# A fused attention and expert-layer kernel: the compressed branch's first product as rows of blocks, and the first loads in another order

## The chip, the cores and the metric

The kernel is one program on one NeuronCore of a Trainium2 chip. The core has five engines with their own instruction streams: TensorE (PE; its weight loads are shown as PEld), VectorE (DVE), ScalarE (ACT), GpSimdE (POOL) and SyncE (SP). They wait for each other by semaphores. DMAs are issued from the queues of SP, ACT and POOL. The metric is the time of one execution on the device, in microseconds (us). Three runs of the kernel before took 2562.18 to 2570.23, with a median of 2567.21.

## The reference, cut to what matters

Two blocks run one after the other on X of 512 tokens x 1024 features, all in float32. The first is attention with three branches and a gated MLP. The second is a short convolution beside a gated recurrence, and then an expert layer: each token picks 128 experts of 16384 and reads their rows of two tables. The change touches the compressed part of the third attention branch. There each of two key/value groups is cut in blocks of 32 tokens with stride 16, and each block goes through a two-layer MLP:

```
def compress_blocks(kv, pe, w1, w2):        # kv: (1, 512, 2, 64)
    n_cmp = (S - 32) // 16 + 1              # 31 blocks
    blocks = kv[:, idx] + pe
    flat = blocks.transpose(0, 1, 3, 2, 4).reshape(1, n_cmp, 2, 32 * 64)
    return jax.nn.gelu(flat @ w1) @ w2      # w1: 2048 x 256, w2: 256 x 64
kc = compress_blocks(k_cmp, cmp_pe, k_w1, k_w2)
vc = compress_blocks(v_cmp, cmp_pe, v_w1, v_w2)
...
merged = g[:, :, 0] * (y_a @ w_pa) + g[:, :, 1] * (y_b @ w_pb) + g[:, :, 2] * (y_c @ w_pc)
```

`kc` and `vc` are then the keys and values of one more attention, and `g` is a sigmoid of a product with 3072 columns of `w_in` (the gates).

## The kernel before, in words

The 512 tokens are worked in two groups, g = 0 and 1, of 256 (two tiles of 128). For each group the program runs `project`, `attend`, `merge`, `mlp`, `mixer` and `queries`. During group 1 the engines also work off the expert steps of group 0: a "job" is one gather of 128 rows of 4 KB by POOL's queue and one pass of DVE over them. The experts of group 1 make up the rest of the program, from about 1780 us on.

Weights stream from memory through a ring of four buffers of 1 MB, W0 to W3, in the order of `weight_tiles`, all from SP's queue. Tile i is asked for when the last use of tile i - 4 is done. X's two tiles for group 0 are loaded by `load_x(0)` as the first DMAs of ACT's queue, then come COLS (biases and gains) and FIX (identity, a row of numbers, two constants). SP issues the first weight tile at once and the others after X is there.

`norm` squares X on ACT (two halves for each tile), takes the root, and PE turns X while it scales it (L660). ACT needs a table of functions for Square and another for Sqrt. The projections follow: a "feature" is eight products of a 128x128 weight with 256 tokens.

`compressed(g)` makes the first product of the MLP. FB holds the blocks in turned form: 128 partitions x 30 columns for each of 16 parts of the 2048 rows (in group 1, 32 columns, and the buffer is XS0). For each of keys and values (kv) and each half m of the 256 hidden columns, 16 products are summed with a 128x128 piece of the weights as the part that stands in the array and FB's 30 columns moving past it; ACT applies the gelu straight into HID, where the hidden index lies on the partitions, as the second product (KCT, VCB) needs it. These 64 products a group all run before (g = 1) or around (g = 0) the first attention unit.

`attend(g)` then goes through 44 units (22 heads x 2 tiles, u = 0 to 43). PE's order at unit u is: scores of u, turning of the probabilities of u - 2, values of u - 3, and then the pieces that the table `BESIDE` puts beside u: a "gate" piece is one feature and a tanh on ACT. The coroutine `compressed` advances one `yield` a unit. In group 1 the expert steps are spread over this by `state["spent"]`: each product adds what it is reckoned to take, and as much expert work is taken off; 5.0 is added for each of the four sums of the compressed product. KEPT = 16 jobs are held back for the end. Each engine works off the same list up to the point that PE's order sets (`catch_up`).

## Time and profile before

| | |
|---|---|
| three runs, median (range) | 2567.21 (2562.18 to 2570.23) us |
| profiled execution, its own time | 2564.7 us |
| its span | 2562.9 us |
| busy: PE, PEld, DVE | 2218.9, 1560.6, 1564.3 us |
| busy: ACT, POOL | 617.7, 943.8 us |
| instructions | 24943 |
| moved by DMA | 683.55 MB, 267 GB/s |

A busy PE is not a PE at its peak: a matmul's end is modelled, and the granted clock (PEclk) says at how much of its full rate the array ran. A float32 product stands in the trace as two records, so "x16" is eight products. PEclk is 1.0 at 2.4 GHz and 0.5 at 1.2 GHz; numbers between are stretches that hold both. The trace shows the instruction's line; L633 is the helper `mm` of all products, so the names of the operands tell them apart.

### The profile page before, as it was taken

To read this page: it belongs to the slowest core of one execution; us is meant where nothing else is said; L and a number is where in the kernel's file an instruction comes from. 1 tells how busy PE (TensorE), PEld (TensorE's weight loads), DVE (VectorE), ACT (ScalarE), POOL (GpSimd) and SP (SyncE) were. 2 spreads that over 40 slices of the span, in tenths; PEclk is the share of its full clock that TensorE was granted. 3 is DMA by queue.
4 is the path that set the end of the run, shared out by engine and by line. 5 is a ranking of instruction groups with operands and counts; after the bars stand their busy time and mean duration, and the time that the engine had idled before them with its cause. 6 is when DMAs were issued, how large, how long until landed. Compare 5 with 4: busy or idle time off the path is not lost.

```text
span 2562.9 us, 24943 instructions
## 1 busy us (share of the span) xinstructions
PE 2218.9 (87%) x8844; PEld 1560.6 (61%) x8844; DVE 1564.3 (61%) x3488; ACT 617.7 (24%) x1763; POOL 943.8 (37%) x772
## 2 busy tenths in 40 slices
PE   7999999999989899998999989778433599999992
PEld 6877768856858777676688637647333544444441
DVE  0122321202436957899777766857989988666667
ACT  1223211202211121432111213111799600000000
POOL 0000000000002534555456564624677246555554
PEclk9979999999989986998999999889655899999996
DMA  5432344444436987898899998957789489999997
GB/s 166 141 99 75 107 140 156 156 148 137 132 98 239 330 283 255 291 323 295 324 337 401 387 399 303 355 198 269 264 305 357 134 325 407 407 409 409 409 409 288
DMA packets 296689, 683.55 MB, mean 267 GB/s; under 512 B 21234, under 2 KB 134130, under 8 KB 296308
## 3 DMA queue, kind: packets, MB, share of 16 engines
q0 software_dynamic: 110592, 402.70, 42.3%
q1 hardware_dynamic: 179904, 266.54, 30.3%
q10 hardware_dynamic: 6068, 12.71, 1.5%
q8 instruction: 70, 1.15, 0.2%
q14 instruction: 55, 0.45, 0.1%
HBM read 679.78 MB, written 2.10 MB: 266 GB/s over the span
## 4 chain that ended last, share of the span: by engine, by line
PE 43%; DVE 25%; DMA 17%; POOL 8%; issue 4%; ACT 2%; ACTq 0%; DVEq 0%; POOLq 0%
PE bank L633 41%; DMA SLOT<-in_peer_v,EI 8%; DVE SLOT L1753 8%; POOL SLOT L2298 8%; DMA SLOT<-in_peer_u,EI 8%; DVE ACC L1767 3%; PE bank L660 2%; DVE X L1767 1%; DVE H L1685 1%; DVE PB L1306 1%; DVE OH L1652 1%; DVE OH L1657 1%; DVE EX L1660 1%; DMA W<-in_cmp_k_w 1%; PE bank L785 1%
## 5 line engine op out<-in xcount | busy, mean ns | idle before, releaser
L2298 POOL DMA_INDIRECT SLOT<-in_peer_u,EI x512 | 640.7, 1251 | 1364.8 <-DVE EI L1669 828.4
L633 PE MATMUL bank<-HT,W 128*128 128x256 f32 x4032 | 917.9, 388 | 16.5 <-issue 6.6
L633 PEld LDWEIGHTS bank<-HT,W 128*128 128x128 f32 x4032 | 776.6, 194 | 136.2 <-issue 17.2
L1753 DVE CUSTOM_DVE_ANT_0 SLOT<-SLOT,H 128x1024 f32<-128x1024 f32 x384 | 454.8, 1221 | 50.7 <-DMA SLOT<-in_peer_u,EI 49.3
L2298 POOL DMA_INDIRECT SLOT<-in_peer_v,EI x256 | 302.9, 1183 | 231.8 <-DVE ACC L1767 96.0
L633 PE MATMUL bank<-H,SPREAD 128*128 128x512 f32 x680 | 302.7, 596 | 7.1 <-DMA H<-in_peer_v 7.0
L633 PEld LDWEIGHTS bank<-H,SPREAD 128*128 128x128 f32 x680 | 125.9, 190 | 178.2 <-issue 133.0
L1767 DVE SCALAR_TENSOR_TENSOR X<-SLOT,AA,X 128x1024 f32<-128x1024 f32 x128 | 164.4, 1284 | 76.9 <-DMA SLOT<-in_peer_v,EI 74.1
L1753 DVE CUSTOM_DVE_ANT_0 SLOT<-SLOT,ACC 128x1024 f32<-128x1024 f32 x128 | 154.5, 1223 | 64.4 <-DMA SLOT<-in_peer_u,EI 64.1
L1767 DVE SCALAR_TENSOR_TENSOR ACC<-SLOT,AA,ACC 128x1024 f32<-128x1024 f32 x128 | 164.1, 1282 | 19.8 <-DMA SLOT<-in_peer_v,EI 13.7
L633 PE MATMUL bank<-JK,SPREAD 128*128 128x512 f32 x344 | 157.1, 599 | 3.6 <-DMA JK<-in_peer_v 3.6
L633 PE MATMUL bank<-W,UT 128*128 128x512 f32 x352 | 151.4, 592 | 0.0
L633 PEld LDWEIGHTS bank<-JK,SPREAD 128*128 128x128 f32 x344 | 63.2, 190 | 93.2 <-issue 65.8
L633 PEld LDWEIGHTS bank<-W,UT 128*128 128x128 f32 x352 | 66.9, 190 | 83.3 <-issue 83.2
L633 PE MATMUL bank<-H 128*128 128x128 f32 x296 | 58.4, 362 | 60.3 <-ACT H L2210 52.2
L633 PE MATMUL bank<-JK 128*128 128x128 f32 x216 | 47.4, 388 | 63.9 <-ACT JK L2210 56.6
L1827 ACT ACTIVATE HT<-X 128x512 f32<-128x512 f32 x40 | 24.9, 624 | 294.0 <-DVE X L1430 150.6
L633 PEld LDWEIGHTS bank<-H 128*128 128x128 f32 x296 | 50.8, 260 | 67.6 <-ACT H L2210 53.2
L1961 ACT ACTIVATE PB<-PB,NM 128x128 f32<-128x128 f32 (+2 forms) x88 | 48.7, 554 | 155.8 <-DVE NM L1306 155.1
L1306 DVE CUSTOM_DVE_ANT_0 PB<-bank,BIAS 128x128 f32<-128x128 f32 (+2 forms) x72 | 34.2, 476 | 84.3 <-PE bank L633 82.3
L633 PEld LDWEIGHTS bank<-JK 128*128 128x128 f32 x216 | 40.8, 282 | 70.3 <-ACT JK L2210 57.8
L660 PE MATMUL bank<-XS,X 128*128 128x128 f32 x256 | 40.7, 334 | 49.2 <-DVE SS L1152 31.8
(304 smaller groups left out, 2389.4 us busy)
## 6 DMA issues: line engine op xcount, KB each, us to landing
W<-in_w_in SPq DMA_DIRECT2D x68, 1024.0 KB, 5.7
W<-in_w_up SPq DMA_DIRECT2D x44, 1024.0 KB, 6.0
H<-in_peer_v SPq DMA_DIRECT2D x85, 512.0 KB, 6.8
JK<-in_peer_v SPq DMA_DIRECT2D x43, 512.0 KB, 6.8
W<-in_w_down SPq DMA_DIRECT2D x20, 1024.0 KB, 6.3
W<-in_peer_wq SPq DMA_DIRECT2D x16, 1024.0 KB, 5.8
W<-in_w_o SPq DMA_DIRECT2D x8, 1024.0 KB, 6.1
W<-in_w_out SPq DMA_DIRECT2D x8, 1024.0 KB, 6.2
```

Source lines behind the costliest of these rows:

```text
L633: return e.matmul(out, lhsT, rhs, start=start, stop=stop)
L660: k = e.matmul(pb[:, c * P:(c + 1) * P], lhsT=X[:, t, at:at + P], rhs=DIAG[t], start=True, stop=True)
L785: k = e.transpose(pb[:, j * P:(j + 1) * P], PB[u % 3][:, j * P:(j + 1) * P], IDENT)
L1306: e.tensor_tensor_reduce(out=PB[u % 3][:, 0:wd], in0=ps("score", g, u)[:, 0:wd], in1=t, scale=-1.0, scalar=3.0e38, op0=ALU.add, op1=ALU.mi ...
L1652: e.tensor_tensor(OH, HL.unsqueeze(2).to_broadcast([P, 64, 16]), IOTA[:, 0:16].unsqueeze(1).to_broadcast([P, 64, 16]), ALU.is_equal).then_inc(
L1657: e.tensor_tensor(one_hot, one_hot, IF.unsqueeze(2).to_broadcast([P, 4, 16, 16]), ALU.mult).then_inc(*d_exp.mark("pick", t, h))
L1660: e.tensor_reduce(EX.rearrange("p l s j -> p (l s j)"), OH, AX, ALU.add).then_inc(*d_exp.mark("add", t, h))
L1685: k = e.tensor_scalar(left[:, i, :], IOTA, TURNED[t][:, 1, n:n + 1], TURNED[t][:, 0, n:n + 1], ALU.is_equal, ALU.mult)
L1753: e.tensor_tensor_reduce(out=x, in0=x, in1=NORMED[t], scale=1.0, scalar=0.0, op0=ALU.mult, op1=ALU.add, accum_out=AA[t % 2][:, k:k + 1]).t ...
L1767: e.scalar_tensor_tensor(SUM[t], x, AA[t % 2][:, k:k + 1], SUM[t], ALU.mult, ALU.add).then_inc(*d_exp.mark("job", t, i))
L1961: e.activation(s, s, ACT.Exp, bias=NM[:, n, il:il + 1], scale=-1.0, accum_out=LS[:, n, il:il + 1]).then_inc(*a_att.mark("exp", g, u))
L2298: e.indirect_dma_start(out=SLOT_OF[s], out_offset=None, in_=a["peer_v_2"] if i >= P else a["peer_u_2"], in_offset=bass.IndirectOffsetOnAxi ...
```

## The change

The first product of the compressed branch is turned round: FB's 30 (32) columns are now what stands in the array, and 256 columns of the weights move past, so one sum of 16 products gives a 30 x 256 result for each kv. ACT's gelu writes it to a new buffer HB, rows of blocks. PE turns it in two pieces of 128 (function `turned`), and ACT copies them into HID. The turning for kv = 0 comes behind the products of kv = 1, the one for kv = 1 a `yield` later, before the second product. The four additions of 5.0 to `spent` are gone.

The eight gates of the first branch stand beside units 0, 1, 2, 4, 6, 8, 11, 15 in place of 1, 4, 6, 8, 10, 13, 16, 19, in both groups.

X's first tiles are issued from SP's queue ahead of the first weight tile. ACT's queue issues FIX and then COLS. ACT takes a root of a 1.0 that DVE writes at its start, before it waits for anything that was loaded.

```diff
@@ -174,7 +174,7 @@
 
 ALPHA = 24
 BESIDE = {}
-for _u, _p in ([(u, ("gate", 0, m)) for m, u in enumerate((1, 4, 6, 8, 10, 13, 16, 19))]
+for _u, _p in ([(u, ("gate", 0, m)) for m, u in enumerate((0, 1, 2, 4, 6, 8, 11, 15))]
                + [(13, ("turned", 0, 0))] + [(21 + m // 2, ("part", 0, m)) for m in range(8)]
                + [(23 + m, ("gate", 1, m)) for m in range(8)] + [(27, ("turned", 1, 0))]
                + [(31 + m // 3, ("part", 1, m)) for m in range(8)]
@@ -398,6 +398,7 @@
         PCT.append(buf("PCT", 2, GB, P, at=at + 384))
         CT.append(buf("CT", 2, GB * 96, at=at + 896))
         CM.append(buf("CM", 2, GB * 96, at=at + 1280))
+        HB = [[buf(f"HB{j}", 256, at=at + 1664 + 256 * j) for j in range(2)]]
         FBF.append(XS[0])
         FW.append(XS[1][:, 0:2 * T].rearrange("p (a b) -> p a b", a=2))
         W2.append([XS[1][:, 512 + 128 * j:640 + 128 * j].rearrange("p (a b) -> p a b", a=2) for j in range(2)])
@@ -405,6 +406,7 @@
         PCT.append(buf("PCT_1", 2, GB, P, at=jk_at + 384))
         CT.append(buf("CT_1", 2, GB * 96, at=nf_at))
         CM.append(buf("CM_1", 2, GB * 96, at=nf_at + 384))
+        HB.append([buf("HB_1", 256, at=nf_at + 768), XS[1][:, 768:1024]])
         BV = XS[0][0:1, 0:914]
 
 
@@ -695,23 +697,33 @@
                 c0, nb = (0, 15) if g == 0 else (15 + 16 * (g - 1), 16)
                 ntot = c0 + nb
                 FB = FBF[g].rearrange("p (a b c) -> p a b c", a=2, b=16)[:, :, :, 0:2 * nb]
+
+                def turned(kv):
+
+                    pb, _ = take(("hidt", g, kv), (a_cmp, ("hidt", g, kv)))
+                    w.wait_ge(*a_cmp["hid", g, kv])
+                    for m in range(2):
+                        k = e.transpose(pb[:, m * 32:m * 32 + 2 * nb], HB[g][kv][0:2 * nb, m * P:(m + 1) * P],
+                                        IDENT[0:2 * nb, 0:2 * nb])
+                    k.then_inc(*p_cmp.mark("hidt", g, kv))
+
                 for kv in range(2):
-                    (i0, w0), (i1, w1) = tile(), tile()
-                    for m in range(2):
-                        pb, _ = take(("hid", g, kv, m), (a_cmp, ("hid", g, kv, m)))
-                        w.wait_ge(*d_cmp["fb", g, 1])
-                        for c in range(16):
-                            k = mm(pb[:, 0:2 * nb], (w0, w1)[c // 8][:, c % 8, m * P:m * P + P], FB[:, kv, c, :],
-                                   c == 0, c == 15)
-                        state["spent"] += 5.0
-                        k.then_inc(*p_cmp.mark("hid", g, kv, m))
-                    last_use(i0, p_cmp, "hid", g, kv, 1)
-                    last_use(i1, p_cmp, "hid", g, kv, 1)
+                    halves = (tile(), tile())
+                    pb, _ = take(("hid", g, kv), (a_cmp, ("hid", g, kv)))
+                    w.wait_ge(*d_cmp["fb", g, 1])
+                    for c in range(16):
+                        k = mm(pb[0:2 * nb, 0:256], FB[:, kv, c, :], halves[c // 8][1][:, c % 8, :], c == 0, c == 15)
+                    k.then_inc(*p_cmp.mark("hid", g, kv))
+                    for i, _ in halves:
+                        last_use(i, p_cmp, "hid", g, kv)
+                    if kv:
+                        turned(0)
                     yield
+                turned(1)
                 w.wait_ge(*cw_in["cw", g, 1])
                 for q in range(2):
                     pb, _ = take(("kct", g, q), (d_cmp, ("kct", g, q)))
-                    w.wait_ge(*a_cmp["hid", g, 1, 1])
+                    w.wait_ge(*a_cmp["hidt", g, 1])
                     lo, hi = q * 31 + c0, q * 31 + ntot
                     mm(pb[0:64, 0:nb], W2[g][0][:, 0, :], HID[:, 0, 0, lo:hi], True, False)
                     mm(pb[0:64, 0:nb], W2[g][0][:, 1, :], HID[:, 0, 1, lo:hi], False, True).then_inc(
@@ -1769,6 +1781,7 @@
                 if k == P - 1:
                     out(t)
 
+            e.memset(SS[:, 31:32], 1.0).then_inc(*d_set.mark("one"))
             for v in (AH, UH, STP, VCB):
                 e.memset(v, 0.0)
             e.memset(ONER[0:1, :], 1.0)
@@ -1911,14 +1924,24 @@
             def compressed(g):
                 c0, nb = (0, 15) if g == 0 else (15 + 16 * (g - 1), 16)
                 ntot = c0 + nb
+
+                def turned(kv):
+                    catch_up("hidt", g, kv)
+                    w.wait_ge(*p_cmp["hidt", g, kv])
+                    for m in range(2):
+                        k = e.copy(HID[:, kv, m, :].rearrange("p (q c) -> p q c", q=2)[:, :, c0:ntot],
+                                   ps("hidt", g, kv)[:, m * 32:m * 32 + 2 * nb].rearrange("p (q c) -> p q c", q=2))
+                    k.then_inc(*a_cmp.mark("hidt", g, kv))
+
                 for kv in range(2):
-                    for m in range(2):
-                        catch_up("hid", g, kv, m)
-                        w.wait_ge(*p_cmp["hid", g, kv, m])
-                        e.activation(HID[:, kv, m, :].rearrange("p (q c) -> p q c", q=2)[:, :, c0:ntot],
-                                     ps("hid", g, kv, m)[:, 0:2 * nb].rearrange("p (q c) -> p q c", q=2),
-                                     ACT.Gelu_apprx_tanh).then_inc(*a_cmp.mark("hid", g, kv, m))
+                    catch_up("hid", g, kv)
+                    w.wait_ge(*p_cmp["hid", g, kv])
+                    e.activation(HB[g][kv][0:2 * nb, :], ps("hid", g, kv)[0:2 * nb, 0:256],
+                                 ACT.Gelu_apprx_tanh).then_inc(*a_cmp.mark("hid", g, kv))
+                    if kv:
+                        turned(0)
                     yield
+                turned(1)
                 yield
                 yield
                 for par in range(2):
@@ -2250,9 +2273,10 @@
                     w.wait_ge(*d_exp["sum", t, 1])
                     out(t)
 
-            load_x(0)
+            e.dma_start(FIX, con("ident", 258)).then_inc(*small_in.mark("fix"))
             e.dma_start(COLS, a["cols"]).then_inc(*small_in.mark("cols"))
-            e.dma_start(FIX, con("ident", 258)).then_inc(*small_in.mark("fix"))
+            w.wait_ge(*d_set["one"])
+            e.activation(SS[:, 30:31], SS[:, 31:32], ACT.Sqrt)
             for t_small in ("cols", "fix"):
                 w.wait_ge(*small_in[t_small])
             for g in range(NG):
@@ -2303,6 +2327,9 @@
 
         def sync(e, real):
             w = Waits(e, real)
+            xv = a["x"].rearrange("(t p) d -> t p d", p=P)
+            for t in range(GB):
+                e.dma_start(X[:, t, :], xv[t]).then_inc(*x_in[t].mark("x", 0, t))
             for i, (parts, width) in enumerate(tiles):
                 if 1 <= i < RING:
                     for t in range(GB):
```

What follows shows how the instructions of the engines moved. First PE at the compressed product of group 0, before (FB is the block buffer, W1 to W3 and W0 are the ring's buffers; the operand that moves stands first, so `FB,W` has the weights in the array):

```order
L633 MATMUL bank0<-FB_109,W1_55 128x30 x8
L633 MATMUL bank0<-FB_109,W2_56 128x30 x8
L633 MATMUL bank1<-FB_109,W1_55 128x30 x8
L633 MATMUL bank1<-FB_109,W2_56 128x30 x8
L810 MATMUL bank2<-FIX_52,FC_63 128x4 x2
L633 MATMUL bank3<-FB_109,W3_57 128x30 x8
L633 MATMUL bank3<-FB_109,W0_54 128x30 x8
L633 MATMUL bank4<-FB_109,W3_57 128x30 x8
L633 MATMUL bank4<-FB_109,W0_54 128x30 x8
L633 MATMUL bank5<-KF_60,QF_97 128x128
L633 MATMUL bank6<-FC_63,SEL_62 128x256
L633 MATMUL bank7<-HID_64,CW0_111 64x15 x2
```

After, the same place up to the second attention unit (HB is the new buffer, FIX holds the identity, CW the second weights, HT,W a gate's feature):

```order
L635 MATMUL bank0<-W1_55,FB_109 30x256 x8
L635 MATMUL bank0<-W2_56,FB_109 30x256 x8
L822 MATMUL bank1<-FIX_52,FC_63 128x4 x2
L635 MATMUL bank2<-W3_57,FB_109 30x256 x8
L635 MATMUL bank2<-W0_54,FB_109 30x256 x8
L706 MATMUL bank3<-FIX_52,HB0_117 128x30 x2
L635 MATMUL bank4<-KF_60,QF_97 128x128
L635 MATMUL bank5<-FC_63,SEL_62 128x256
L635 MATMUL bank6<-HT_50,W1_55 128x256 x8
L706 MATMUL bank7<-FIX_52,HB1_118 128x30 x2
L635 MATMUL bank0<-HID_64,CW0_111 64x15 x2
L635 MATMUL bank1<-HID_64,CW0_111 64x15 x2
```

64 products of 30 moving columns became 32 of 256, two pairs of turnings were added, and a gate's feature stands between the first unit's scores and the second turning.

ACT at the start of the program, before:

```order
L2179 DMA X_49<-in_x 128x1024 x2
L2254 DMA COLS_51<-in_cols 128x219
L2255 DMA FIX_52<-in_con 128x258
L1827 ACT_TABLE_LOAD
L1827 ACTIVATE HT_50,SS_53<-X_49 128x512 x2
L1835 ACTIVATE SS_53<-SS_53,FIX_52 128x1 x2
L1837 ACT_TABLE_LOAD
L1837 ACTIVATE SS_53<-FIX_52 128x1
```

ACT at the start, after:

```order
L2276 DMA FIX_52<-in_con 128x258
L2277 DMA COLS_51<-in_cols 128x219
L2279 ACT_TABLE_LOAD
L2279 ACTIVATE SS_53<-SS_53 128x1
L1840 ACTIVATE HT_50,SS_53<-X_49 128x512 x2
L1848 ACTIVATE SS_53<-SS_53,FIX_52 128x1 x2
L1850 ACTIVATE SS_53<-FIX_52 128x1
```

One of the two table loads is gone, and the other stands ahead of the squares of X; X's own DMA is no longer ACT's.

ACT around the same place of group 0, after (in the order before, four ACTIVATE HID<-bank rows of 128x2x15 stood there, and the first gate behind the second unit's exponential):

```order
L1939 ACT_TABLE_LOAD
L1939 ACTIVATE HB0_117<-bank0 30x256
L1972 ACTIVATE BIAS0_99<-DIST_98,FIX_52 128x256
L1939 ACTIVATE HB1_118<-bank2 30x256
L1932 COPY HID_64<-bank3 128x2x15 x2
L1984 ACT_TABLE_LOAD
L1984 ACTIVATE PB0_101,LS_91<-PB0_101,NM_90 128x128
L2062 ACTIVATE GATE_107<-bank6,COLS_51 128x256
L1932 COPY HID_64<-bank7 128x2x15 x2
L1984 ACTIVATE PB1_102,LS_91<-PB1_102,NM_90 128x256
```

Two gelus on 30 x 256 and four copies take the place of four gelus on 128 x 30, and the second pair of copies stands behind the first gate.

## Rows read from the trace of the kernel before

**Rows 1.** Timeline, the first 16 us: start us, us, engine line op [idle before]

```profile
9.56 1.28 ACT L1827 ACT_TABLE_LOAD   x1 [9.56 <-DMA FIX<-in_con]
...
12.57 1.28 ACT L1837 ACT_TABLE_LOAD   x1
13.87 0.20 ACT L1837 ACTIVATE SS<-FIX 128x1 f32<-128x1 f32 x1
...
15.58 0.16 DVE L1152 RECIPROCAL SS<-SS 128x1 f32<-128x1 f32 x1 [5.41 <-ACT SS L1842]
```

**Rows 2.** DMA issues from 0 to 20 us: KB each, median us to landing

```profile
X<-in_x ACTq DMA_DIRECT2D x2, 512.0 KB, 5.9
...
FIX<-in_con ACTq DMA_DIRECT2D x1, 129.0 KB, 7.2
```

**Rows 3.** Timeline, PE, 117 to 153 us

```profile
117.71 11.01 PE L633 MATMUL bank<-FB,W 128*128 128x30 f32 x64
...
128.96 13.86 PE L633 MATMUL bank<-FB,W 128*128 128x30 f32 x64
...
146.73 6.00 PE L633 MATMUL bank<-HT,W 128*128 128x256 f32 x16
```

**Rows 4.** Stretches: busy us (x) of PE, PEld, DVE, ACT, POOL, granted clock, DMA share, GB/s

```profile
117.00:143.00 26.00, 26.00 (x139) 25.86 (x138) 0.17 (x1) 4.21 (x9) 0.00 (x0) 0.57 0.47 145
143.00:165.00 22.00, 21.57 (x84) 15.98 (x85) 7.58 (x35) 5.63 (x19) 0.00 (x0) 0.66 0.30 96
165.00:200.00 35.00, 32.18 (x142) 24.47 (x141) 8.90 (x46) 12.48 (x47) 0.00 (x0) 0.84 0.19 61
200.00:250.00 50.00, 49.50 (x241) 39.09 (x240) 13.54 (x68) 18.38 (x68) 0.00 (x0) 0.97 0.28 83
...
980.00:1010.00 30.00, 26.91 (x83) 16.93 (x84) 25.42 (x72) 5.87 (x16) 10.04 (x9) 0.61 0.66 221
1010.00:1200.00 190.00, 175.59 (x791) 129.59 (x789) 180.30 (x496) 63.72 (x163) 100.92 (x84) 0.91 0.86 296
```

**Rows 5.** Timeline, ACT taking a feature off PE

```profile
34.09 0.47 ACT L1894 ACTIVATE KF<-bank,COLS 128x256 f32<-128x256 f32 x1 [2.98 <-PE bank L633]
```

**Rows 6.** Timeline, PE with 4 columns of the array in use

```profile
83.62 2.32 PE L633 MATMUL bank<-HT,W 128*4 128x256 f32 x10
```

**Rows 7.** Timeline, group 1: SP's issue, PE's products, DVE's wait

```profile
939.30 7.01 SPq L2314 DMA_DIRECT2D W<-in_cmp_v_w  x2
...
950.03 27.49 PE L633 MATMUL bank<-XS,W 128*128 128x32 f32 x128 [5.51 <-DMA W<-in_cmp_k_w]
977.90 1.01 PE L633 MATMUL bank<-HID,XS 128*64 128x16 f32 x8 [0.38 <-ACT HID L1918]
978.52 0.78 DVE L1225 COPY KCT<-bank 64x16 f32<-64x16 f32 x4 [10.60 <-PE bank L633]
```

**Rows 8.** DMA issues from 938 to 948 us: KB each, median us to landing

```profile
W<-in_cmp_v_w SPq DMA_DIRECT2D x2, 1024.0 KB, 18.7
```

**Rows 9.** Timeline at the end of the mixer of group 1

```profile
1696.70 29.86 PE L633 MATMUL bank<-W,MIX 128*128 128x512 f32 x64 [9.32 <-DVE O L1567]
...
1716.29 0.69 DVE L1407 TENSOR_TENSOR X<-X,bank 128x512 f32<-128x512 f32 x1 [18.03 <-PE bank L633]
```

**Rows 10.** The stretch behind that idle time, in the columns of rows 4

```profile
1696.00:1701.00 5.00, 4.30 (x5) 1.85 (x6) 2.19 (x5) 0.00 (x0) 0.94 (x1) 0.50 0.15 30
```

**Rows 11.** The page, part 5, a job on DVE: busy, mean ns, idle before

```profile
L1753 DVE CUSTOM_DVE_ANT_0 SLOT<-SLOT,H 128x1024 f32<-128x1024 f32 x384 | 454.8, 1221 | 50.7 <-DMA SLOT<-in_peer_u,EI 49.3
```

**Rows 12.** Timeline, PE, group 0: the gates at units 13 and 19

```profile
197.59 6.14 PE L633 MATMUL bank<-HT,W 128*128 128x256 f32 x16
...
215.21 3.67 PE L633 MATMUL bank<-HT,W 128*128 128x256 f32 x16
```

**Rows 13.** Timeline, ACT, group 1: the gates at units 13 and 19

```profile
1061.67 0.47 ACT L2039 ACTIVATE KF<-bank,COLS 128x256 f32<-128x256 f32 x1 [2.72 <-PE bank L633]
...
1085.19 0.47 ACT L2039 ACTIVATE KF<-bank,COLS 128x256 f32<-128x256 f32 x1
```

## The prediction

> **What bounds the kernel now.** I read the stretches of the timeline first, then the chain of waits, then the timeline of single places. The reader should see that the change touches three places and that another thing sets the pace in each.
>
> At the start PE has nothing to do until ACT has squared X. ACT is idle until FIX has landed, loads a table at 9.56, a second one at 12.57, and DVE gets the roots at 15.58 [rows 1]. In group 0 PE is busy all the time from 117 to 143, but at a granted clock of 0.57, and until 200 the clock is 0.66 and 0.84 [rows 4]. Here PE alone sets the end: DVE and ACT are busy for less than 8 of 22 us from 143 to 165. In group 1 the same products stand behind a wait for their weights, and DVE, which has the expert jobs to do, has run out of them and waits 10.60 us for the second product [rows 7]. From 1010 to 1200 DVE is busy for 180.30 of 190 us [rows 4]: there DVE is the bound, and PE's gains count only if DVE starts sooner.
>
> **The start.** X and FIX are what ACT waits for. X took 5.9 us to land (the mean of two), FIX 7.2 us though it has a quarter of the bytes, since it was issued behind X and beside the first weight tile [rows 2]. Afterwards FIX goes first on ACT's queue and X first on SP's, ahead of the weight tile. The rows bound when both are there: not before X's 5.9 us (I take 6.6 us on the clock, since the second half of X is issued half a us later), and not after 9.56. The squares then start at about 6.6 in place of 10.85 (9.56 and 1.28 and their overlap), and the table load at 12.57, which holds the row behind it to 13.87, goes: 4.25 + 1.3 = 5.5 us. The new load waits for nothing but DVE's first write and lies beside the DMAs. The least is that FIX comes no sooner and only both loads go from the path, 2.6 us; the most is 7. SP's tiles 1 to 3 still wait for X, which is sooner there, and PE needs tile 0 at about 18, so no weights are late.
>
> The Trainium skill (ScalarE: Activation LUTs, What ACT_TABLE_LOAD costs) gives about 2.66 us for a switch of tables, half of it a drain. By that the two loads would be worth 5.3 us. Here the ACTIVATE behind the load at 12.57 starts 1.30 us later [rows 1], so the trace does not bear the drain out, and the sum goes by 1.3. The skill (Trainium Kernel Development and Optimization, Key Constraints) also says that DMAs from SP's and ACT's queues share the same 16 engines and interleave, so that another queue by itself brings X no sooner. By that alone the squares would start where FIX lands, and only the order of issue would help; the trace has no row that parts the two.
>
> **The product, group 0.** 64 products go, which ran from 117.71 to 142.8: 25.05 us, 0.39 us each, with the products for CQ between them [rows 3]. 32 with 256 moving columns come. The price of one at full clock is a feature's: ACT waits 2.98 us for one and works on it for 0.47, so one comes off every 3.45 us, eight products, 0.431 us each [rows 5]. That is 13.8 us; the columns standing in the array are 30 and not 128, and a feature with only 4 of them takes no less or more (ten records in 2.32 us, two a product, make 0.46) [rows 6]. Added are four turnings of 30 rows (0.25 us, bounded by the 0.39 us of an old product each, and nothing), CQ (0.2), and a wait of about 0.6 us at the second product, since the turning of kv = 1 needs a copy on ACT that stands behind a gate. 25.05 - 13.8 - 0.25 - 0.2 - 0.6 = 10.2 us. The weights of kv = 1 come in 5 to 6 us when nothing else loads, as X did [rows 2], and kv = 0 takes 6.9, so no wait appears. The gelu on ACT, 256 wide, is hidden behind the products of kv = 1 and then behind the gate at unit 0.
>
> **The clock after it, group 0.** The old products hold the clock down and it stays down: the first gate takes 6.00 us [rows 3] where a later one takes 3.67 [rows 12]. Full-clock work lost is length times (1 - clock): 22 x 0.34 = 7.5 us, then 35 x 0.16 = 5.6, then 50 x 0.03 = 1.5, 14.6 together [rows 4]. With dense products before it and gates beside units 0, 1 and 2 the first stretch should stay at full clock; the second dip comes from units with little work between gates, and there the gates are now farther apart. I take 5 us of the 14.6. The ends are 9.6 more, if all comes back, and a loss (below).
>
> **The product, group 1.** The second tile of v's weights is issued last at about 944.5 (939.30 + 7.01 less its own 1.76) and lands 18.7 us later [rows 7, 8], at about 963.5. PE starts kv = 0 at 950.0 behind 5.5 us of idleness. After the 9.32 us of idleness at 1696.70 the clock was at 0.50 for 5 us [rows 9, 10]; the 32 products of 512 columns took 29.86 us, and at 0.862 each (twice a product of 256) they would have taken 27.6: 2.2 us lost. So kv = 0 takes 6.9 + 2.2 and is done at 959.1, PE waits for the tile to 963.5, kv = 1 ends at 972.6, and with turnings and their wait (1.1) the second product starts at 973.7 in place of 977.90: 4.2 us of the 27.5. DVE's wait of 10.60 us takes this up, so DVE starts the attention of group 1 as much sooner. PE's stretch 980 to 1010 at clock 0.61 [rows 4] gets better too; DVE is busy for 25.42 of 30 us there, so I give it 1.5. Together 5.7, with 0 and 12 as ends.
>
> **Expert jobs.** With 5.0 x 4 gone from `spent`, the order of DVE has 5 fewer jobs before KCT, and stays 5 or 6 behind up to the end of the mixer of group 1, where they are done at once. DVE waited 18.03 us there [rows 9]; six jobs of 1.22 us [rows 11] are 7.3. Cost nothing, and 7.3 us plus a landing if the cover were gone. The gates cost the same work as before.
>
> **The sum.** 5.5 + 10.2 + 5 + 5.7 = 26.4 us off the profiled execution's 2564.7: 2538.3. The median of the three runs is 2.5 us above that execution, within their own spread, so 2538. The expert tail from 1780 on does the same work, only sooner.
>
> **Rivals.**
> 1. The array's clock looks at how much of the array works, and 30 of 128 columns are too few: the product runs at 0.5. The four-column feature speaks against it, but it is 3.45 us long. Group 0: 27.5 + 1.05 in place of 25.05, 3.5 slower and no better clock behind; group 1: kv = 1 ends where it did, 0.8 slower. With the start: 2564.7 - 5.5 + 3.5 + 0.8 = 2563.5, no change.
> 2. Only group 0's product and the start count: the clock falls again in the attention as it did between 165 and 200, and in group 1 a busier DMA or DVE takes the rest. 2564.7 - 15.7 = 2549.
> 3. The clock stays full through the attention of group 0: 9.6 more, 2529.
> 4. Slower: the bare units. Units 12 to 20 now have one gate (15) among them. If the clock falls there and stays down, PE's work in them doubles. In group 0 units 14 to 19 took from 203.7 to 218.9 [rows 12], 15.2 us, and 1.3 a unit without their two gates of 3.67: nine units cost 11.8, and the gate 2.5 as at 197.59, 14.3. In group 1 the six units between the gates at 13 and 19 took 23.5 us [rows 13], 2.7 a unit without gates: 24.3 and 2.5, 26.8. In place of gains of 5 and 1.5: 2538.3 + 6.5 + 41.1 = 2586. It decides only if PE loses some 34 us against the forecast, most of these 47.6. For it: the clock of 0.84 from 165 to 200, with gates two or three units apart. Against it: from 200 on it was 0.97 with the same spacing, and DVE hides part of PE's in group 1.
>
> **Chances.** Forecast 0.47, rival 1 0.09, rival 2 0.20, rival 3 0.18, rival 4 0.06. A measurement of this kernel can tell about 0.3%, 7.7 us, from no change. The forecast and rivals 2 and 3 are faster, 0.85; rival 1 is no change, 0.09; slower 0.06. Range 2526 to 2556: it holds rivals 2 and 3 with their own spread and leaves out 1 and 4.
>
> **What would show it.** The roots at about 10 us; the 30x256 products of group 0 in 14 us at clock 1.0 with the first gate at 3.5 to 3.7 us; in group 1 a gap in PE before kv = 1, and DVE's wait for KCT shorter; six jobs together near the end of the mixer. I am wrong if the 30x256 products take 0.86 us each, if X lands after 9 us, or if the stretch of units 12 to 20 is at clock 0.5.

## The result, and the profile after

The changed kernel takes 2547.03 us in the median of six runs (2535.46 to 2551.59), the kernel before 2568.2. The ratio is 0.9913, with a 95% interval of 0.9888 to 0.9937: 22 us less, 16 to 29. The forecast was 2538 in a range of 2526 to 2556. So the sign and the range held; the forecast took 26.4 us off the profiled execution, and 22 came between the medians. The two profiled executions lie 13.1 us apart.

The profiled execution of the changed kernel took 2551.59 us and has a span of 2549.8. Part 1 of its page:

```profile
PE 2194.9 (86%) x8724; PEld 1523.0 (60%) x8724; DVE 1563.9 (61%) x3489; ACT 614.6 (24%) x1765; POOL 958.5 (38%) x772
```

PE is busy for 24 us less than before, and DVE for as long. The start, in the timeline of the changed kernel:

```profile
1.67 1.28 ACT L2279 ACT_TABLE_LOAD   x1 [1.67 <-PEq L2391]
2.96 0.20 ACT L2279 ACTIVATE SS<-SS 128x1 f32<-128x1 f32 x1
7.13 0.63 ACT L1840 ACTIVATE HT<-X 128x512 f32<-128x512 f32 x1 [3.96 <-DMA COLS<-in_cols]
...
10.44 0.16 DVE L1164 RECIPROCAL SS<-SS 128x1 f32<-128x1 f32 x1 [2.75 <-ACT SS L1855]
```

Its DMA issues from 0 to 20 us (KB each, median us to landing):

```profile
X<-in_x SPq DMA_DIRECT2D x2, 512.0 KB, 5.1
...
FIX<-in_con ACTq DMA_DIRECT2D x1, 129.0 KB, 4.7
COLS<-in_cols ACTq DMA_DIRECT2D x1, 109.5 KB, 5.9
```

The roots are there at 10.44 in place of 15.58 [rows 1]. FIX lands in 4.7 us, not 7.2 [rows 2]; the last that the squares wait for is now COLS. The new product of group 0, PE's timeline:

```profile
112.15 7.09 PE L635 MATMUL bank<-W,FB 128*30 128x256 f32 x32
...
119.39 7.09 PE L635 MATMUL bank<-W,FB 128*30 128x256 f32 x32
126.41 0.30 PE L706 MATMUL bank<-FIX,HB 30*128 30x30 f32 x2
...
127.68 3.72 PE L635 MATMUL bank<-HT,W 128*128 128x256 f32 x16
...
132.22 0.61 PE L635 MATMUL bank<-HID,CW 128*64 128x15 f32 x8 [0.58 <-ACT HID L1932]
```

16 products take 7.09 us, 0.443 each, and the first gate behind them 3.72 us where it took 6.00 [rows 3]. The stretches of the changed kernel, in the columns of rows 4:

```profile
112.00:127.00 15.00, 15.00 (x72) 7.43 (x70) 0.17 (x1) 4.33 (x9) 0.00 (x0) 1.00 0.82 244
...
145.00:165.00 20.00, 19.22 (x84) 14.62 (x85) 7.20 (x36) 7.67 (x30) 0.00 (x0) 0.83 0.17 53
165.00:200.00 35.00, 33.17 (x149) 24.62 (x148) 7.69 (x46) 17.05 (x66) 0.00 (x0) 0.85 0.19 61
...
960.00:990.00 30.00, 29.68 (x106) 19.43 (x106) 27.74 (x72) 6.00 (x16) 15.93 (x12) 0.78 0.78 257
990.00:1180.00 190.00, 167.33 (x756) 122.85 (x754) 175.14 (x479) 63.16 (x162) 96.73 (x83) 0.90 0.83 287
```

The granted clock is 1.00 where it was 0.57 [rows 4], but it still falls to 0.83 and 0.85 in the attention of group 0. Group 1, timeline of the changed kernel, from PE's product to DVE's copy and then the end of the mixer:

```profile
936.42 9.05 PE L635 MATMUL bank<-W,XS 128*32 128x256 f32 x32 [5.93 <-DMA W<-in_cmp_k_w]
947.69 7.07 PE L635 MATMUL bank<-W,XS 128*32 128x256 f32 x32 [2.21 <-issue]
...
956.05 0.61 PE L635 MATMUL bank<-HID,XS 128*64 128x16 f32 x8 [0.46 <-ACT HID L1932]
956.46 0.73 DVE L1237 COPY KCT<-bank 64x16 f32<-64x16 f32 x4 [8.32 <-PE bank L635]
...
1696.57 0.69 DVE L1419 TENSOR_TENSOR X<-X,bank 128x512 f32<-128x512 f32 x1 [11.00 <-PE bank L635]
```

DVE's wait for the second product is 8.32 us (10.60 in [rows 7]), and its wait at the end of the mixer 11.00 (18.03 in [rows 9]): the six expert jobs are done there.

To see where the time went, I take the start of one and the same operation in each trace and subtract its time in the first profile of the kernel before. Two profiles of the changed kernel stand here (the second is the run "again" of the experiments), and a second one of the kernel before:

| mark (time in the first profile of before) | before, 2nd | changed | changed, 2nd |
|---|---|---|---|
| PE's first turning of X (16.21) | -0.0 | -5.1 | -5.3 |
| first scores of group 0 (142.75) | -0.0 | -16.1 | -16.9 |
| first `YT,W` product, unit 21 (220.95) | -2.7 | -22.6 | -24.7 |
| mixer of group 0 (663.32) | -2.7 | -19.9 | -21.6 |
| last part of the projection, group 1 (912.52) | -3.2 | -14.0 | -20.7 |
| first product, group 1 (950.03) | -2.3 | -13.6 | -20.8 |
| DVE's KCT copy, group 1 (978.52) | -2.3 | -22.1 | -29.1 |
| X behind the attention, group 1 (1272.66) | -2.9 | -20.6 | -28.9 |
| end of the mixer, group 1 (1716.29) | -2.6 | -19.7 | -28.3 |
| expert steps of the last tiles (2182.61) | -2.3 | -13.9 | -25.4 |
| last norm (2546.98) | -0.2 | -13.1 | -24.8 |

Up to the mixer of group 1 the second profile is 28 us ahead, 2 more than the forecast's 26.4. The first one loses 6 us in the projection of group 1. PE waits there for weights, 3.85 us in all, as its timeline says:

```profile
866.32 10.63 PE L635 MATMUL bank<-HT,W 128*128 128x256 f32 x48 [1.31 <-DMA W<-in_w_in]
879.50 10.76 PE L635 MATMUL bank<-HT,W 128*128 128x256 f32 x42 [2.54 <-DMA W<-in_w_in]
```

Behind the second wait the granted clock is 0.50 from 879.0 to 882.4, which costs 1.7 us more. In the second profile one such wait of 0.61 us stands there. Both give back time behind 1716: 6.6 and 3.4 us.

The second profile of the kernel before is itself 2.7 us ahead of the first one from unit 21 on, without any change. A difference of that size in one column of the table is not yet an effect.

### The profile page after: what moved, and what is told of

Its sections match the earlier page's. It is cut to its first block, busy times and chain, and to the rows that moved or that the text cites. A ratio compares the mean times of both kernels' runs of the same rounds, so it can differ in the third digit from the quotient of the medians.

```text
span 2549.8 us, 24714 instructions
## 1 busy us (share of the span) xinstructions
PE 2194.9 (86%) x8724; PEld 1523.0 (60%) x8724; DVE 1563.9 (61%) x3489; ACT 614.6 (24%) x1765; POOL 958.5 (38%) x772
## 4 chain that ended last, share of the span: by engine, by line
PE 42%; DVE 26%; DMA 17%; POOL 9%; issue 4%; ACT 2%; DVEq 0%; ACTq 0%; POOLq 0%
PE bank L635 40%; POOL SLOT L2322 9%; DVE SLOT L1765 9%; DMA SLOT<-in_peer_v,EI 8%; DMA SLOT<-in_peer_u,EI 7%; DVE ACC L1779 3%; PE bank L662 2%; DVE X L1779 1%; DVE H L1697 1%; DMA W<-in_w_in 1%; DVE PB L1318 1%; DVE OH L1669 1%; DVE OH L1664 1%; DVE EX L1672 1%; DMA W<-in_cmp_k_w 1%
## 5 line engine op out<-in xcount | busy, mean ns | idle before, releaser
L2322 POOL DMA_INDIRECT SLOT<-in_peer_u,EI x512 | 658.7, 1287 | 1334.3 <-DVE EI L1681 807.5
L1765 DVE CUSTOM_DVE_ANT_0 SLOT<-SLOT,H 128x1024 f32<-128x1024 f32 x384 | 454.1, 1222 | 52.2 <-DMA SLOT<-in_peer_u,EI 50.9
L1779 DVE SCALAR_TENSOR_TENSOR ACC<-SLOT,AA,ACC 128x1024 f32<-128x1024 f32 x128 | 164.1, 1282 | 19.9 <-DMA SLOT<-in_peer_v,EI 14.5
L635 PE MATMUL bank<-W,HT 128*128 128x256 f32 (+3 forms) x384 | 83.0, 370 | 0.0
```

Of the source, the lines that this page charges most:

```text
L635: return e.matmul(out, lhsT, rhs, start=start, stop=stop)
L1765: e.tensor_tensor_reduce(out=x, in0=x, in1=NORMED[t], scale=1.0, scalar=0.0, op0=ALU.mult, op1=ALU.add, accum_out=AA[t % 2][:, k:k + 1]).t ...
L1779: e.scalar_tensor_tensor(SUM[t], x, AA[t % 2][:, k:k + 1], SUM[t], ALU.mult, ALU.add).then_inc(*d_exp.mark("job", t, i))
L2322: e.indirect_dma_start(out=SLOT_OF[s], out_offset=None, in_=a["peer_v_2"] if i >= P else a["peer_u_2"], in_offset=bass.IndirectOffsetOnAxi ...
```

## The experiments

Theory: the terms add up as forecast (start, product of group 0, clock behind it, product of group 1), and what is missing at the end is lost to transfers in the projection of group 1 and in the expert steps. Rivals: single parts bring nothing or less; or the missing 9 us are the work of one part. The kernels ran in three groups, each beside runs of the kernel before, whose median was 2575.91 us in the first (start_only, product_only, gates_only, no_gates), 2566.56 in the second (again, gates_by_group, spent, before_again) and 2576.95 in the third (x_queue, early_table, fix_first, spent_gone). The first and the third group ran on one chip, the second on another, and the second profile of the kernel before was taken on the second. All marks are differences from the first profile of the kernel before, whose chip is not on record, so a mark late in the program can hold a difference between chips as well.

**The parts alone.** The start alone:

```diff
+            e.memset(SS[:, 31:32], 1.0).then_inc(*d_set.mark("one"))
...
-            load_x(0)
+            e.dma_start(FIX, con("ident", 258)).then_inc(*small_in.mark("fix"))
             e.dma_start(COLS, a["cols"]).then_inc(*small_in.mark("cols"))
-            e.dma_start(FIX, con("ident", 258)).then_inc(*small_in.mark("fix"))
+            w.wait_ge(*d_set["one"])
+            e.activation(SS[:, 30:31], SS[:, 31:32], ACT.Sqrt)
...
+            for t in range(GB):
+                e.dma_start(X[:, t, :], xv[t]).then_inc(*x_in[t].mark("x", 0, t))
```

> The kernel before with the start alone changed (X on SP's queue ahead of the weights, FIX first on ACT's queue, the early root). Parts add up: PE's first turning at 11.1 us in place of 16.2, everything later moved by 5.6 us, and the time 5.5 us shorter, a ratio of 0.998. Rival, that stretches paced by DMA give part of a gain in group 0 back: the first turning is as early, the mixer of group 0 starts 5.6 us sooner, but less than 3 us is left at the end.

Measured: 2574.47 us, ratio 0.9995 (0.9979 to 1.0011). The first turning is at 10.94, 5.3 us sooner, and the mixer of group 0 10.5 us sooner; but at the last part of the projection of group 1 only 4.5 are left, and from 1811 to 2183 another 16 us are lost. All eight kernels profiled on this chip lose 5 to 16 us there, the ones with the smallest edits too. The gain at the start is shown; what of it reaches the end can't be told from these times.

Of the 10.5 us, 2.4 have nothing to do with the start: the old product of group 0 took 22.6 us in this profile and 25.0 in the first one of the kernel before. The timeline of start_only, PE, up to 117.2 us, and then the second half of the product:

```profile
111.72 5.66 PE L633 MATMUL bank<-FB,W 128*128 128x30 f32 x50
...
120.57 13.86 PE L633 MATMUL bank<-FB,W 128*128 128x30 f32 x64
```

and its stretches, in the columns of rows 4:

```profile
111.70:117.20 5.50, 5.50 (x52) 5.50 (x51) 0.00 (x0) 3.28 (x5) 0.00 (x0) 1.00 0.70 222
117.30:134.30 17.00, 17.00 (x81) 16.92 (x80) 0.17 (x1) 0.79 (x3) 0.00 (x0) 0.50 0.45 143
```

The product begins at the full granted clock, where 25 products take 5.66 us, 0.226 each, and falls to half while PE is busy without a break; then they take 0.433. In the first profile of the kernel before the fall comes 3.0 us into the product, here 5.6, in spent_gone 6.0; the whole takes 22.3 to 25.0 us in eight profiles. At 0.226 each all 64 would take 14.5 us, an estimate, and the 32 new ones take 14.2. So at the same clock the two forms cost the same, and what the new form wins in group 0 is the clock that it keeps. Which of its traits keeps it, the 256 moving columns, the 30 in the array or the fewer products, no run here parts.

The compressed product alone (the hunks of `compressed` and the buffers HB, with the additions to `spent` gone):

> The kernel before with the compressed product alone changed (rows of blocks, turned, and the additions to spent gone). Parts add up: the products of group 0 take 14.2 us in place of 24.9, the first scores come 10.5 us sooner, the dip of the clock behind them is shorter by 3 to 5 us, so 14 to 15 us at the start of the MLP of group 0 and 14 us at the end, ratio 0.9945. Rival, that DMA-paced stretches give gains back: 14 us at the MLP, 8 us or less at the end.

Measured: 2557.35 us, ratio 0.9935 (0.9914 to 0.9957), 17 us less. The product of group 0 gives 10.5 us against the first profile (from -0.9 at its start to -11.5 at the first scores), the mixer of group 0 is at -12.4, and in group 1 the product gives 8.4 (from -6.8 to -15.2). It is the one part whose time by itself is clear of the scatter. Its profiled execution was one of its slowest, 2567.26 us. PE's timeline of that kernel shows the product at full rate and the first gate behind it, which here stands at unit 1, partly at half:

```profile
116.79 7.09 PE L635 MATMUL bank<-W,FB 128*30 128x256 f32 x32
...
135.18 5.41 PE L635 MATMUL bank<-HT,W 128*128 128x256 f32 x16
```

The gates alone, and the changed kernel with the old table of gates (the same edit undone):

```diff
-for _u, _p in ([(u, ("gate", 0, m)) for m, u in enumerate((1, 4, 6, 8, 10, 13, 16, 19))]
+for _u, _p in ([(u, ("gate", 0, m)) for m, u in enumerate((0, 1, 2, 4, 6, 8, 11, 15))]
```

> The kernel before with the table of gates alone changed. If the clock is set by what PE did just before: the old product leaves the clock at half, the gates at units 0, 1 and 2 run at half (6 us each) and nothing is won, 0 us, within 3. Rival, that early gates by themselves bring the clock back: 4 us less at the start of the MLP. Rival of the bare units: units 12 to 20 at half clock, 5 to 15 us more at the start of the MLP of group 0.

Measured: 2580.22 us, ratio 1.0018 (0.9999 to 1.0038). The first gate runs at half the rate, as expected, the second and third not:

```profile
141.42 6.03 PE L633 MATMUL bank<-HT,W 128*128 128x256 f32 x16
...
148.57 3.72 PE L633 MATMUL bank<-HT,W 128*128 128x256 f32 x16
...
153.98 3.62 PE L633 MATMUL bank<-HT,W 128*128 128x256 f32 x16
```

At the mixer of group 0 the kernel is 5.5 us ahead, 3 more than the second profile of the kernel before. But 3.2 of them are there at the first scores, ahead of every gate, again since the clock fell later in the old product (22.8 us). Behind the scores it gains 2.3 us, and six other profiles with the old product and the old table gain 1.0 to 2.9 there. So the expectation of nothing held in group 0, and the first rival did not. In the attention of group 1 the kernel loses 7.9 us (from -5.5 at KCT to +2.4 at X).

> The changed kernel with the old table of gates. If the gates hold the clock up behind the new product: 16.1 us of gain at the first scores as in the changed kernel, but a longer dip, 16 to 18 us at the start of the MLP of group 0 in place of 20.3, and some 3 us slower at the end than the changed kernel (2550). Rival, that the dense product alone is what keeps the clock: 20 us at the MLP with either table and the same time, 2547.

Measured: 2552.36 us, ratio 0.9911 (0.9884 to 0.9937), the changed kernel's ratio. By the marks the table does what the theory says in group 0: -16.7 at the first scores, as with the new table, and -17.4 at the mixer in place of -19.9 and -21.6. That is 2.5 to 4 us. From the first scores to the mixer the two kernels with the new product and the old table (product_only and this one) gain 0.9 and 0.7 us, the four profiles with the new product and the new table (changed, twice, spent and gates_by_group) 3.0 to 4.7. No time of a run can tell it.

The three parts alone give ratios whose product is 0.995, and all together give 0.991. The intervals are too wide to say that the difference is real. product_only and no_gates differ by the start alone, and their medians by 5.0 us, which is what the start should be worth; their intervals overlap.

**Is the loss behind group 0 the change's?**

> The changed kernel once more, on the chip of the experiments' kernels. If what it lost behind its first profile (6.3 us in the projection of group 1, 7 us in the expert steps at the end) is a matter of the single execution: at the same marks up to the queries of group 0 it stands within 1 us of the first profile, behind them the difference scatters by several us, and the ratio is again 0.991 within 0.003. Rival, that the change causes both losses: they are there again, 5 to 7 us each, at the same places.

Measured: 2542.7 us, ratio 0.9915 (0.9894 to 0.9936). In group 0 the two profiles lie up to 2.1 us apart (I expected 1), behind it 12. The loss in the projection is gone, the one in the expert steps is 3.4 in place of 6.6. So the 6 us in the projection belong to single executions: they stand in the first profile, in start_only, product_only and spent, that is in four of the seven profiles that are 10 us or more ahead at the mixer of group 0, and in none of the seven others, the two of the kernel before among them. That hints that being early makes them likelier; it does not show it.

> The kernel before, profiled once more on this chip. If the traces of the experiments scatter behind the queries of group 0 for reasons that have nothing to do with the change, this one does too: up to there within 3 us of the first profile, in the expert steps from 1880 us on 10 to 15 us later. Rival, that every changed kernel is slow there and this one is not: within 3 us to the end.

Measured: 2564.48 us. It stays within 3.7 us of the first profile at every mark and ends 0.2 us from it. The rival held for this kernel's two profiles. It does not clear the kernel before of scatter on the other chip, where its median is 10 us higher and no profile of it was taken.

**The additions to `spent`.** The changed kernel with the additions kept:

```diff
                     for c in range(16):
                         k = mm(pb[0:2 * nb, 0:256], FB[:, kv, c, :], halves[c // 8][1][:, c % 8, :], c == 0, c == 15)
+                    state["spent"] += 10.0
```

> The changed kernel with the additions to spent kept (10.0 for each kv), so that as many expert jobs as before stand before DVE's copy for the second product of group 1. Forecast's theory: the jobs are hidden wherever they stand; DVE would have 5 more jobs (6 us) before KCT, which take up its wait there, and the same end, within 2 us of the changed kernel. Rival: DVE is late for KCT by some us and group 1 ends 3 to 6 us later. Second rival: the five jobs fewer before it are missing later, and keeping them makes it 2 to 4 us faster.

Measured: 2551.61 us, ratio 0.9930 (0.9911 to 0.9949), 9 us above the changed kernel in the same group of runs, though the intervals overlap. The profile is plain. Timeline of this kernel, PE and DVE at the second product of group 1:

```profile
959.44 0.63 PE L635 MATMUL bank<-XS,HID 128*31 128x64 f32 x8
...
968.79 2.77 PE L635 MATMUL bank<-KCT,QF 64*128 64x31 f32 x12 [8.50 <-DVE KCT L1238]
```

```profile
968.01 0.72 DVE L1238 COPY KCT<-bank 64x16 f32<-64x16 f32 x4
```

DVE copies KCT without having waited, and PE waits 8.50 us for it. In the second profile of the changed kernel DVE waits in the same place:

```profile
949.44 0.73 DVE L1237 COPY KCT<-bank 64x16 f32<-64x16 f32 x4 [8.03 <-PE bank L635]
```

From the start of the first product of group 1 to the end of the mixer the changed kernel gains 6.1 and 7.5 us in its two profiles, this one 1.9. The first rival holds. At the end of the mixer DVE waits 18.94 us here:

```profile
1701.61 0.69 DVE L1420 TENSOR_TENSOR X<-X,bank 128x512 f32<-128x512 f32 x1 [18.94 <-PE bank L635]
```

and 11.00 in the changed kernel: the jobs taken away before KCT stand in an idle time there, for nothing. The same edit on the old product:

```diff
-                        state["spent"] += 5.0
```

> The kernel before with only the four additions to spent gone (the old product). DVE waited 10.60 us for the second product in group 1 there, so fewer jobs ahead of it make that wait longer and win nothing: the second product at the same time, 977.9 within 1 us, and a ratio of 1.000 within 0.002. Rival, that moving expert jobs behind the attention's start helps by itself: DVE's copy KCT earlier or the attention of group 1 shorter by 3 us or more, and the ratio 0.998 or less.

Measured: 2574.95 us, ratio 1.0003 (0.9981 to 1.0026); KCT at -2.7, as in the second profile of the kernel before (-2.3). With the old product the edit is worth nothing, since DVE waited for PE anyway. From the start of the first product to the end of the mixer, product and edit together gain 6.1 and 7.5 us, the product without the edit 1.9, and the edit without the product loses 2.0.

**The new gates in group 0 only** (group 1 with the old table):

```diff
+GATES0 = ((0, 1, 2, 4, 6, 8, 11, 15), (1, 4, 6, 8, 10, 13, 16, 19))
+for _u, _p in ([(u, ("gate", 0, m, g)) for g in range(2) for m, u in enumerate(GATES0[g])]
```

> The changed kernel with the new table of gates in group 0 and the old one in group 1. Theory: in group 0, where PE sets the end, early gates win 2.5 us by the start of the mixer; in group 1, where DVE does, they cost 4 to 8 us of the attention. So group 0 as in the changed kernel, the attention of group 1 4 us shorter, and the time 4 us less than the changed kernel. Rival, that the difference in group 1 is chance: the same time as the changed kernel, within 2 us.

Measured: 2543.06 us, ratio 0.9903 (0.9887 to 0.9919). From KCT to X both this kernel and the second profile of the changed one lose 0.2 us: the 4 us that I laid to the table in group 1 do not appear, and my theory fell. The eight other profiles with the old table in group 1 lie there between a gain of 3.0 and a loss of 2.7 us; the 7.9 of gates_only alone stand outside, in one profile, and stay open. It is not a better version. Its trace shows the scatter of the expert steps best: level with the second profile of the changed kernel at 1811 us (-28.4 and -29.3), 12 us behind it at 2183. From 1880 to 2000 us, groups by line, POOL and DVE of this kernel:

```profile
L2324 POOL DMA_INDIRECT SLOT<-in_peer_u,EI x65 | 88.9, 1368 | 28.1 <-issue 16.5 <-DVE AA L1767 9.2 <-DVE I L1634 0.3
L1767 DVE CUSTOM_DVE_ANT_0 SLOT<-SLOT,H 128x1024 f32<-128x1024 f32 x60 | 71.7, 1222 | 15.8 <-DMA SLOT<-in_peer_u,EI 15.3
```

and of the changed kernel's second profile:

```profile
L2322 POOL DMA_INDIRECT SLOT<-in_peer_u,EI x65 | 78.8, 1212 | 40.4 <-DVE AA L1765 22.4 <-issue 15.5 <-DVE SCORED L1626 0.3
L1765 DVE CUSTOM_DVE_ANT_0 SLOT<-SLOT,H 128x1024 f32<-128x1024 f32 x59 | 70.5, 1222 | 7.7 <-DMA SLOT<-in_peer_u,EI 6.7
```

One pass of DVE takes 1222 ns in both; one gather's issue on POOL takes 1368 ns in the one and 1212 in the other, 10 us over 65 of them, and DVE waits 15.3 us for gathers in place of 6.7. Why POOL is slower in one execution stays open.

**The start taken apart.** Three edits of the kernel before, each profiled once.

x_queue moves the loads alone:

```diff
-            load_x(0)
+            e.dma_start(FIX, con("ident", 258)).then_inc(*small_in.mark("fix"))
             e.dma_start(COLS, a["cols"]).then_inc(*small_in.mark("cols"))
-            e.dma_start(FIX, con("ident", 258)).then_inc(*small_in.mark("fix"))
...
+            for t in range(GB):
+                e.dma_start(X[:, t, :], xv[t]).then_inc(*x_in[t].mark("x", 0, t))
```

> The kernel before with the queues alone changed: X first on SP's queue, FIX and then COLS on ACT's, both table loads where they were. Forecast's parts: the small tables are there at about 7.1 us in place of 9.6, but the load for Square then stands behind them (1.3 us) and the load for Sqrt lies in between (1.3 us), so PE's first turning at 11.1 + 2.6 = 13.7 us. Rival, that the loads were hidden beside X's landing: 12.4 us or less.

early_table adds the root alone:

```diff
+            e.memset(SS[:, 31:32], 1.0).then_inc(*d_set.mark("one"))
...
             e.dma_start(FIX, con("ident", 258)).then_inc(*small_in.mark("fix"))
+            w.wait_ge(*d_set["one"])
+            e.activation(SS[:, 30:31], SS[:, 31:32], ACT.Sqrt)
```

> The kernel before with the early root alone (the loads of X, COLS and FIX as before, W0 beside them). Forecast's parts: FIX still lands at 9.6 us, the squares start there, and both table loads go from the path: PE's first turning at 16.2 - 2.6 = 13.6 us. Rival, that one load alone counts: 14.9 us.

fix_first has the root too, and FIX ahead of X on ACT's queue:

```diff
+            e.dma_start(FIX, con("ident", 258)).then_inc(*small_in.mark("fix"))
             load_x(0)
             e.dma_start(COLS, a["cols"]).then_inc(*small_in.mark("cols"))
-            e.dma_start(FIX, con("ident", 258)).then_inc(*small_in.mark("fix"))
```

> The kernel before with the early root and FIX issued first, but X and COLS behind it on ACT's queue and SP's first weight tile at once, as before. If queues share the same engines and only what is issued first counts: X lands beside W0 and COLS behind X at about 9 us, the squares wait for COLS, and the first turning is at 13 us, close to early_table. Rival, that the order on ACT's queue is what counts and W0 beside it costs nothing: squares at 7.1 us and the turning at 11.1, as with X on SP's queue.

Measured: the first turning at 12.44, 13.47 and 13.44 us (before 16.21, all parts of the start together 10.94). In x_queue the rival held: the load for Square lies beside X and COLS and costs nothing, the one for Sqrt stands on the path. Timeline of x_queue, ACT:

```profile
5.34 1.28 ACT L1827 ACT_TABLE_LOAD   x1 [5.34 <-DMA X<-in_x]
7.07 0.63 ACT L1827 ACTIVATE HT<-X 128x512 f32<-128x512 f32 x1 [0.44 <-DMA COLS<-in_cols]
...
8.79 1.28 ACT L1837 ACT_TABLE_LOAD   x1
```

In early_table both loads go from the path, 2.7 us. In fix_first the squares wait for COLS instead of FIX, at the same time as before; timeline of fix_first:

```profile
9.49 0.63 ACT L1828 ACTIVATE HT<-X 128x512 f32<-128x512 f32 x1 [4.98 <-DMA COLS<-in_cols]
```

FIX lands in 3.9 us there, but X takes 6.9 and COLS 7.1. So FIX ahead of X brings nothing by itself. The other 2.5 us, from 13.44 to 10.94, come with X on SP's queue: the first weight tile is then issued behind X and not beside it, and COLS ahead of X and not behind it. These runs do not part the two: COLS ahead of X with the tile still beside it was not run. The Trainium skill says that queues share the 16 engines (Trainium Kernel Development and Optimization, Key Constraints). These runs agree: X took 5.1 us with the weight tile behind it, and with the tile beside it 5.9, or 6.9 where FIX went ahead of X too.

## Why the prediction was right, and what was mis-sized

The median of 2547 lies 9 us from the forecast's 2538 and 2 us from rival 2's 2549. Rival 2's mechanism did not hold all the same: group 1 gave its gain, and up to the end of its mixer the second profile is 28.3 us ahead. The time came near rival 2 by losses behind group 0 that neither had. The 28.3 is measured from the first profile of the kernel before; from the second it is 25.7. That the terms add up so well is in part luck, as the bullets on the clock and on group 1 show.

- **Start, 5.5 us**: right, 5.1 and 5.3 at the first turning, 5.7 and 6.4 at the first feature. The squares start at 7.13 (forecast 6.6), held by COLS, which the forecast did not name. The parts are not 4.25 and 1.3, though: each of the two edits by itself gives 3.8 and 2.7, because the load for Square goes from the path by either of them, and counts once. The ACTIVATE follows the load at 1.67 after 1.29 us, and the two loads were worth 2.7 us in early_table. With the drain that the Trainium skill adds (ScalarE: Activation LUTs, What ACT_TABLE_LOAD costs) they would be worth 5.3, an estimate; the 2.7 measured here do not agree with it.
- **Product of group 0, 10.2 us**: right against the first profile, 10.5 in three profiles of the new product; against the other seven of the old one it is 7.8 to 10.4. The forecast set 0.39 us of an old product against 0.431 of a new one as if both were prices. The 0.39 is a mixture of 0.226 and 0.433, by when the clock fell, and at the full clock the old form costs as little as the new. The array held 30 columns at a clock of 1.00: rival 1 is out. The wait at the second product was 0.58 us, forecast 0.6.
- **Clock behind it, 5 us**: 3.8 and 4.7 us from the first scores to the mixer, against the first profile. Six other profiles with the old product and the old table gain 1.0 to 2.9 us on that stretch, so the 14.6 us of lost clock that the forecast started from were a high case, and against the median of the six, 2.8, the term is worth 1 to 2 us. It was too large. What there is comes with the new gates: without them the new product gains 0.7 and 0.9. Rival 3 is out: the clock falls again to 0.83 and 0.85. Timeline of the changed kernel behind the last gate, unit 15:

```profile
192.69 1.02 PE L635 MATMUL bank<-KF,QF 64*128 64x256 f32 x2
...
198.40 3.73 PE L635 MATMUL bank<-YT,W 128*128 128x256 f32 x8
...
203.50 1.95 PE L635 MATMUL bank<-YT,W 128*128 128x256 f32 x8
```

The clock falls in the bare units, at about 193, and is back at 203, behind the first part at unit 21: 3.73 us for that one and 1.95 for the later ones. The kernel is 22.6 us ahead at unit 21 and 20.3 at the first gate of the second branch (228.53 before): 2.3 us, not the 41 of rival 4. The kernel before has such a fall as well, with its gates closer together: its gate at 197.59 took 6.14 us [rows 12]. So the bare units did not bring a new one.
- **Product of group 1, 5.7 us**: the first product was worth 8.4 and 8.3 us up to KCT. The term of 4.2 was mis-sized at kv = 1: I let it wait for its weights until 13.5 us behind the start and then run for 9.1 us. It waited until 11.3 us (2.21 us of wait in place of 4.4) and ran for 7.1 at full clock. The 1.5 us given for the stretch behind it did not come: up to X 1.5 and 0.2 us were lost again. The two errors go against each other.
- **Expert jobs, "cost nothing"**: right as far as it went, as the wait of 11.00 us shows, but the forecast did not see that the term of group 1 hangs on this edit. With the additions kept DVE would have been 8.5 us late for KCT.
- **"The expert tail does the same work, only sooner"**: here the missing time went, beside the 6 us in the projection of one profile. From the end of the mixer to the last norm the changed kernel lost 6.6 and 3.4 us; the second profile of the kernel before lost 2.4. Of the other kernels those on its chip lost 2.8 (spent) and 14.8 (gates_by_group), and the eight on the other chip 6.5 (early_table) to 14.8 (product_only). With the 6 us in the projection the first profile ends 13.1 us ahead, without them the second 24.8, and the 22 us of the medians lie between. Whether a program that is ahead by 28 us meets these transfers worse for that reason, or by chance, stays open: gates_by_group and again, with the same marks up to there, lost 14.8 and 3.4.

## What to carry to other kernels

Look at the granted clock before reading a price off a product. 64 products with 30 moving columns took 22 to 25 us because the clock fell to half inside them; at the full one they would have taken 14.5, an estimate from the 0.226 us each ahead of the fall. Turned round, so that the long side moves and the short side stands in the array, 32 products with 256 columns took 14.2 us and kept the clock at full. When an engine's work is shortened beside another engine that fills its waits with other work, the filler has to be cut by as much, or the gain turns into a wait on the other side (8.50 us here). And a gain that is won before a stretch of gathers should be counted with what such a stretch scatters: the time of a run does not settle a part of 3 us. The marks of a trace do so only when several profiles agree, since the kernel before differs from itself by 2.7 us within group 0.

## What the runs showed of the hardware

- The same changed kernel, profiled twice, differs by 12 us at the end; up to 810 us the two differ by about 2 at most.
- POOL's issue of one gather took 1212 ns in one execution and 1368 in another, over the same 65 of them.
- The kernel before has a median of 2566.56 us on one chip and of 2575.91 and 2576.95 in two groups on another, so that only ratios within one group are compared.
- The granted clock fell from 1.00 to 0.50 in the old product while PE was busy without a break (17.00 of 17.00 us at 0.50 in start_only), 3.0 us into it in one profile and 6.0 in another. With 30 columns in the array and 256 moving it stayed at 1.00 for the whole 15 us.
- A float32 product with 128 x 128 in the array and 30 moving columns took 0.226 us at the full clock and 0.433 at half (start_only); one with 128 x 30 in the array and 256 moving columns took 0.443 at the full clock (the changed kernel).
